# Where the z_s product stands in each round of a state-space stage

## What is computed

```python
proj = h @ w_in[l]
u_s, z_s, q_lat, kv_lat, k_rope, z_m, gl_s, gl_m = jnp.split(proj, split_at, axis=-1)
y_s = _ssm_branch(u_s, ...)
glu_a, glu_b = jnp.split(jax.nn.gelu(y_s) @ w_glu[l] + b_glu[l], 2, axis=-1)
y_s = ((glu_a * jax.nn.sigmoid(glu_b)) * jax.nn.silu(z_s)) @ w_br_ssm[l]
```

## Time and profile before

| what | value |
|---|---|
| median of three runs | 2168.73 us |
| profiled execution, its time | 2164.7 us |
| profiled execution, its span | 2163.0 us |
| TensorE busy | 1976.5 us, 91% of the span |
| VectorE, ScalarE, GpSimd busy | 1067.0, 855.5 and 203.9 us |
| mean granted TensorE clock | 0.926 of full speed |
| rounds 1 to 6 of the state-space stage | 1381.5 to 1562.0 us from the start of the span |
| round 7 | 1562.0 to 1580.0 us |

### The profile page before, as it was taken

How to read it: one execution, slowest core, us unless ns; L and a number is a source line. 1 busy time by engine, 2 the same in 40 slices (tenths; PEclk the granted TensorE clock), 3 DMA queues, 4 the chain that set the end, 5 groups by cost and what they waited for, 6 DMA issues and landing times. The chain is left out here.

```text
span 2163.0 us, 33020 instructions
## 1 busy us (share of the span) xinstructions
PE 1976.5 (91%) x12904; PEld 1784.9 (83%) x12904; DVE 1067.0 (49%) x1506; ACT 855.5 (40%) x1135; POOL 203.9 (9%) x337
## 2 busy tenths in 40 slices
PE   5999999999999996999999966688898999999996
PEld 4999999999999885999999945577776777778884
DVE  4444434444333237455441278856446676764443
ACT  4555455555322134333332242122236656553331
POOL 0110000010000000000000008565200000000000
PEclk8999999899899998999999988676689999999998
DMA  3211221211222341222322237121121121223332
GB/s 112 74 64 58 68 68 58 78 58 58 78 88 87 108 131 53 89 87 87 91 94 88 69 122 111 32 50 42 40 83 54 54 78 53 83 78 107 117 108 87
DMA packets 74871, 170.15 MB, mean 79 GB/s; under 512 B 31152, under 2 KB 31280, under 8 KB 74672
## 3 DMA queue, kind: packets, MB, share of 16 engines
q1 hardware_dynamic: 74800, 169.17, 25.8%
HBM read 156.30 MB, written 10.49 MB: 77 GB/s over the span
## 5 line engine op out<-in xcount | busy, mean ns | idle before, releaser
L1572 DVE TENSOR_TENSOR WL<-WR,WH 128x1024 fp32r<-128x1024 f32 x271 | 331.9, 1225 | 320.9 <-ACT WH L1144 312.7
L710 PE MATMUL J<-XH,WH 128*128 128x264 f32 x1728 | 366.3, 294 | 18.9 <-DVE XL L1576 18.9
L1144 ACT ACTIVATE WH<-WR 128x1024 fp32r<-128x1024 f32 x271 | 284.2, 1052 | 230.8 <-PE J L892 85.2
L710 PE MATMUL J<-XL,WH 128*128 128x264 f32 x1728 | 361.4, 291 | 0.0
L710 PE MATMUL J<-XH,WL 128*128 128x264 f32 x1728 | 360.2, 291 | 0.0
L710 PEld LDWEIGHTS J<-XH,WH 128*128 128x128 f32 x1728 | 278.0, 195 | 22.9 <-issue 17.3
L710 PEld LDWEIGHTS J<-XL,WH 128*128 128x128 f32 x1728 | 277.5, 195 | 0.0
L710 PEld LDWEIGHTS J<-XH,WL 128*128 128x128 f32 x1728 | 276.5, 195 | 0.0
L2193 POOL TENSOR_SCALAR_AFFINE_SELECT E<-E 128x128 f32<-128x128 f32 (+1 forms) x160 | 45.0, 319 | 501.5 <-DVE E L1622 345.5
L922 PE MATMUL J<-X2H,WH 128*128 128x512 f32 x168 | 77.4, 461 | 10.0 <-DVE X2L L1850 8.7
L2215 POOL TENSOR_TENSOR SM<-SM 128x32 f32<-128x32 f32 x15 | 4.6, 308 | 748.5 <-DVEq L1884 747.4
(11 more groups left out here) (408 smaller groups left out, 4368.5 us busy)
## 6 DMA issues: line engine op xcount, KB each, us to landing
WR<-weights SPq DMA_DIRECT2D x271, 512.0 KB, 3.5
X<-tokens SPq DMA_DIRECT2D x4, 528.0 KB, 5.7
H<-tokens SPq DMA_DIRECT2D x1, 2112.0 KB, 7.7
res_dram<-H SPq DMA_DIRECT2D x1, 2048.0 KB, 8.1
u_dram<-UT SPq DMA_DIRECT2D x8, 256.0 KB, 2.2
US<-u_dram SPq DMA_DIRECT2D x16, 128.0 KB, 6.9
y_dram<-YT SPq DMA_DIRECT2D x8, 256.0 KB, 2.2
YF<-y_dram SPq DMA_DIRECT2D x64, 32.0 KB, 1.8
```

The costliest lines, as they stand in the source:

```text
L710: mm = pe.matmul(o[:, 512 * h:512 * h + HALF], ws[:, s, w], xs[:, k * L1 + h * HALF:k * L1 + (h + 1) * HALF], start=(k == 0 and i == 0), s ...
L1144: act.activation(WH[:, n % SPLIT, :], WR[:, n % RAW, :], ACT.Copy).then_inc(w_hi, 1)
L1572: dve.tensor_tensor(WL[:, n % SPLIT, :], WR[:, n % RAW, :], WH[:, n % SPLIT, :].bitcast(F32), ALU.subtract).then_inc(w_lo, 1)
```

## The change

In each round the z_s job moves behind the state products and ahead of the output products, on TensorE. On ScalarE the Silu that reads it moves behind `y_back` and `kernel_out`. Three turns of state products and the z_s turn exchange numbers: in round `m` (1 to 6) the state products have turns 5m+3 to 5m+5 in place of 5m+4 to 5m+6, and z_s has 5m+6 in place of 5m+3. In round 0 z_s has turn 6 in place of 0. Round 7 keeps its order and its turns on TensorE. No instruction is added or removed, and the programs of VectorE, GpSimd and SyncE keep their order.

```diff
 def t_zs(m):
-    return T_SSM + 3 + 5 * m if m else T_SSM
+    return T_SSM + (5 * m + 6 if m < DT - 1 else 5 * m + 3)
 def t_turned(m):
-    return T_SSM + 5 * m - 1 if m else T_SSM + 1
+    return T_SSM + 5 * m - 2 if m else T_SSM
...
             for m in range(DT):
-                job2(N_SSM + m, t_zs(m), X2H, X2L)
                 if m == 0:
                     states_in(0)
                 if m + 1 < DT:
                     states_in(m + 1)
+                job2(N_SSM + m, t_zs(m), X2H, X2L)
                 t = t_y(m)
...
             for m in range(DT):
                 split_hi(N_SSM + m + 3)
-                src = result2(N_SSM + m, t_zs(m))
-                act.activation(SZS[:, m * S2:(m + 1) * S2], src, ACT.Silu).then_inc(read_out[t_zs(m) % 2], 1)
                 if m == 0:
                     kernel_out(0)
                 if m:
                     y_back(m - 1)
                 if m + 1 < DT:
                     kernel_out(m + 1)
+                src = result2(N_SSM + m, t_zs(m))
+                act.activation(SZS[:, m * S2:(m + 1) * S2], src, ACT.Silu).then_inc(read_out[t_zs(m) % 2], 1)
                 t = t_y(m)
```

## The result

The changed kernel takes 2186.32 us (median of 5 runs, 2184.27 to 2196.03), the kernel before 2170.62 us (median of 5, 2163.92 to 2173.71). The ratio is 1.0087, with an interval from 1.0058 to 1.0116: the change costs 0.9%, 13 to 25 us. It is slower, as forecast, and inside the range; the forecast of 2199 us, +30 us, was 11 to 14 us too high, so that the change costs half to two thirds of what was forecast.

What follows compares the result with a forecast made beforehand. Bound: TensorE's rounds, placed by the DMA chain through YF, which covered z_s. Rounds 1 to 6 add 23.8 us, round 0 6.3 us: +30.1 us on the 2168.7 us median, forecast 2199 us, range 2184 to 2211 us.

Steps and rivals of the forecast that it cites:

- The cover and its loss: Rounds 1 to 6: z_s, hidden in the 15.1 us DMA chain through YF, becomes uncovered; removing it there gains nothing.
- The rival in which BT is ready earlier: Rounds 1 to 6: L965 starts at about 12.6 us instead of 15.1 us; +15 us, 2184 us; chance 0.05.
- The term that was mis-sized: Rounds 1 to 6: the z_s job between L965 and the output products adds 7.58 us a round.
- they start at the slow clock and become fast midway: The moved z_s matmuls, rounds 1 to 6: mean clock 0.69 to 0.80, length 7.58 us.
- The signs named in advance: Profile after: z_s jobs 6.8 to 7.9 us, output products 8.8 to 10.4 us, rounds 33 to 35 us.
- Small matmuls at the slow clock: Head of a round: about 3.4 us instead of 1.7 us, ending at 12.6 us, before L965; no cost.
- The output products: Rounds 1 to 6, behind z_s: 9.57 us, the mean of rounds 7 and 0, a gain of 3.62 us each.
- The rival in which they stay fast to their end: Output products take 7.6 us a round; in all +16 us, 2185 us; chance 0.10.
- The rival in which they get nothing: Output products stay at 13.28 us, +8.0 us a round; in all +58 us, 2226 us; chance 0.10.
- The rival on the other side: Clock pays for everything: z_s 5.46 us, output products 7.6 us; 2167 us, no change; chance 0.05.
- the fast pace of 0.95 us: Output products at full clock: 0.95 us per two groups, eight such pairs making 7.6 us.
- Round 0: z_s uncovered behind L965 for 5.46 us, output products 8.77 to 9.57 us; together +6.3 us.

Runs made afterwards that it cites:

- the two exchanges: Two edits of the kernel before: ScalarE's kernel_out ahead of y_back, 2124.33 us (ratio 0.9783); SyncE's TK issues behind those of YF, 2167.09 us (0.9991).
- the exchange: ScalarE's kernel_out(m + 1) put ahead of y_back(m - 1) in the kernel before: 2124.33 us, ratio 0.9783.
- the second profile: The changed kernel measured once more in another execution, without an edit: 2184.69 us, ratio 1.0077 against the kernel before.

## Why the prediction was right, and where it was off

**The cover and its loss: right.** z_s was hidden in the chain through YF (cutting it in the order of before gains nothing), and in the new order L965 comes no earlier, 14.6 to 15.8 us after the output products against 14.6 to 15.7 us. That the chain runs through ScalarE's order and SyncE's TK issues is shown by the two exchanges, each of which brings L965 to 11.2 us. What the prediction didn't say is that the pause ahead of L965 was needless: it took the order of ScalarE as given. The rival in which BT is ready earlier didn't come about by the change; with the exchange it does.

**The term that was mis-sized is the z_s job.** The prediction took 7.58 us, the mean of jobs that began at the slow clock behind 13 us of output products. In the new place they take 6.54 us. The step that failed is "they start at the slow clock and become fast midway": two of six jobs in the first profile, and three in the second, run at full clock from start to end in 5.6 us, since the clock is already up at L965, and the other four of the first profile take 7.0 us on average. This is 6.2 us of the 7.3 us by which the six rounds were overestimated (+16.5 us for +23.8 us). The others nearly cancel: the output products gain 20.1 us for 21.7 us predicted, L965 gains 1.2 us and the way to it 1.6 us, for nothing predicted. The signs named in advance miss in the same place: z_s jobs of 5.6 to 7.4 us for 6.8 to 7.9 us, and three of six rounds of 30 to 32 us for 33 to 35 us. Small matmuls at the slow clock, 3.4 us in the prediction, are in the trace at 0.43 us spacing for eight groups, and still done before L965.

**The output products: right in kind and size.** 9.86 us on average for 9.57 us, in a spread from 8.9 to 11.0 us for 8.8 to 10.4 us. That the averages lie so close is partly luck: the 8.77 us that went into the 9.57 us came from round 0, where no z_s job stood directly ahead and where the other kernels of that order took 10.9 to 11.2 us. The rival in which they stay fast to their end is out: no profile of any kernel here has them below 8.5 us. With it goes, for these small matmuls, what the Trainium skill's page "TensorE: Matmul & The Clock Gate", section "Why this matters for your kernels", leads one to expect of back-to-back matmuls. Here they are issued without a pause and the granted clock still falls to 1.2 GHz, some 3 to 6 us after the first of them in each of the eight rounds of the changed kernel. The rival in which they get nothing is out too, in the full kernel; with z_s cut to three matmuls it holds in four of six rounds. The rival on the other side needed both the z_s job and the output products fast to their end in nearly every round; the first half came true in two of six rounds (three in the second profile), the second never.

**The unit of a count was wrong, without effect.** The trace has two instructions for each output product, so the fast pace of 0.95 us holds for one group, where the prediction wrote two; the eight of them that it added up to 7.6 us are the eight groups. By the same count the "32 matmuls" of `US` with `BT` are 16 in the program, two for each group, and 32 instructions in the trace. And in the earlier trace rows the stretch of round 3 begins 0.10 us behind its first output product (1456.60 us), so that it took 12.84 us and not 12.74 us, which moves the gain by 0.02 us a round.

**Round 0: right by luck.** +7.1 us in the profiles compared, +6.3 us predicted; but the 8.77 us from which both start was a lucky execution, and +4.5 us is nearer.

**The total.** The stage costs +23.3 and +20.3 us in two profiles against the one of before, and the runs say +15.5 to +19 us, with intervals that reach from 10 to 25 us over both comparisons. Taken alone, 2186 us lies nearer to the rival of output products fast to their end (2185 us) and to that of an earlier BT (2184 us) than to the forecast of 2199 us; only the traces tell them apart, and they show neither. The profiled execution of before was a fast one (2164.7 us, the median being 2170.6 us), with a lucky round 0. The remaining few us are within the spread between executions, and weren't followed further.

**What stays open.** The way to L965 varies from 14.6 to 16.2 us where YF places it; in the profile of before the issues of the YF loads take 3.64 us in some rounds and 4.6 to 4.7 us in others, and in round 6 it is the issues of TK that take 6.12 us in place of 5.08 us. Why they do wasn't tried. Nor was it tried what spreads the start of the stage between executions, from 1325.0 us (z_s cut, in the order of before) to 1339.3 us (the changed kernel), with the same program ahead of it.

## What to carry to other kernels

When a product is taken out from under a wait, ask first whether that wait is itself needed: here one ScalarE copy queued behind another copy's DMA was worth 44 us, and moving the covered work about cost 15 to 19 us. Price a moved job with the clock that it will find and the clock that it leaves behind; here a 6.5 us job gave back 3.5 us by warming what stood next to it, and cutting it to an eighth saved nothing. And compare a stage in its own stretch, with more than one profile: the whole span of this pair agreed with the forecast through 7.8 us of chance.

## What the runs showed of the hardware that wasn't expected

TensorE issued the output products (64 columns each, three matmuls per group) without a pause, and in all of the rounds in which they began at 2.4 GHz (76 of the 96 in the twelve profiles) the granted clock fell to 1.2 GHz under them: 3.7 us after the dense job's end in round 7 of before, and with a dense matmul of 512 columns ahead of each group as well. Twice as much dense work ahead didn't delay the fall (output products 10.27 us for 9.86 us). Thirteen matmuls whose result nobody reads, in a pause that was there anyway, made a kernel of 2168 us 24 us faster.
